# Layer 0's softmax in a two-model transformer kernel: order of evacuations, of ScalarE's shares and of the bias load

## The chip, the cores and the metric

The kernel runs on one core of a Trainium2 chip. TensorE (PE) multiplies matrices into PSUM banks, VectorE (DVE) and ScalarE (ACT) do elementwise work, GpSimd (POOL) does small work and issues some transfers, SyncE (SP) issues most transfers. All transfers share 16 DMA engines. The metric is device time of one launch in microseconds (us); a profiled execution gives the trace.

## The reference

Two small transformers run one behind the other on one sequence of 256 tokens of width 1024, two layers each. The change lies in the attention of the very first layer, so only this matters:

```python
c_act = jax.nn.silu(c)
for l in range(DEPTH):                       # DEPTH = 2
    mod = c_act @ ada_w[l] + ada_b[l]        # (1, 1024) @ (1024, 6144)
    shift_m, scale_m, gate_m, shift_f, scale_f, gate_f = ...   # six rows of 1024
    h = rms_norm(x, g_pre_mix[l]) * (1.0 + scale_m) + shift_m
    proj = h @ w_in[l] + b_in[l]             # 1280 columns: q, k, v, u
    q, k, v, u = ...                         # q and k rotated
    attn_out = sliding_window_attention_with_sinks(q, k, v, sinks[l])   # 8 heads, 2 kv heads, window 128
    pool_out = causal_pool_mixer(u, pool_w[l], pool_scale[l])
    mix = jnp.concatenate([attn_out, pool_out], axis=-1) @ w_out[l]
    x = x + gate_m * rms_norm(mix, g_post_mix[l])
    h = rms_norm(x, g_pre_ffn[l]) * (1.0 + scale_f) + shift_f
    f = (jax.nn.silu(h @ w_gate[l]) * (h @ w_up[l])) @ w_down[l]
    x = x + gate_f * rms_norm(f, g_post_ffn[l])
```

## The kernel before

Every engine has its own program, written out by hand in the order in which it is to run. Engines meet only at semaphores: `sig(name, key)` counts one up, and `wait_ge(*due(name, key))` waits for it. Nothing is reordered by a scheduler, so an instruction that waits holds up everything behind it on its engine.

**Modulation units.** A row of modulation is a product of a vector with a matrix. VectorE does it. A unit `("ada", l, n)`, called (l,n) in the text, is 256 columns of `ada_w[l]`, 1 MB, held transposed in one slot of `raw_w`; `ada(l, n)` is two instructions at L1641, each multiplying 128 columns by `c_row` and summing them (the accumulator is read by a short extra record). After n = 11, 15 and 19 a column of eight tiles is put together (L1658 and L1663 or L1664) and signals `modcol`: gate of the mixer, shift and scale of the feed-forward. For layer 0 the units come in the order (0,4) (0,0) (0,5) (0,1) (0,6) (0,2) (0,7) (0,3), then 8, 9, 10, 11, 16, 17, 18, 19, 12, 13, 14, 15, and behind them the feed-forward's weights ("gu",0,0), ("gu",0,1) and so on.

**The ring of weights.** `raw_w` has four slots. SP loads the units in this order (L1034), and before a load it waits until the unit four places earlier is done. Behind some units it also loads slices of the input weights (`ink`, L1040) and the four tiles of the output weights (`whole`, L1038: tile 2 behind (0,9), 3 behind (0,10), 0 behind (0,17), 1 behind (0,19)).

**Input products.** For every one of eight feature tiles, VectorE scales the turned input (L1842, `scaled0`), tiles 6 and 7 after (0,3). TensorE (L705) multiplies it with the input weights into six banks, (T, c) with T the half of the tokens and c a group of columns: c = 0 has 512 (q and k), c = 1 has 256, c = 2 has 512 (values and pooled features). Slices 0 to 5 go over all six banks in turn, then the last two slices product by product: (0,0) (1,0) (0,1) (1,1) (0,2) (1,2), with the transposes of the rotated q and k between (L546). VectorE adds the bias and moves each product out (`evacuate(L, T, c)`, L1853, for c = 0 and 1 with the rotation, L1863 to L1866). The scores (L504) are written to the two banks that products (0,2) and (1,2) leave.

**The bias row** `bias` (in tile `shared`, 640 KB over 128 partitions) is loaded by POOL, on a DMA queue of its own, with three small loads behind it.

**Softmax.** Six blocks of scores, n = 0 to 5. `scored(n)` on VectorE scales and masks (L1787) and takes the extreme (L1790, `smax`); `exps(n)` on ScalarE takes exponents and sums (L1301); `over_sum(n)` on VectorE takes the reciprocal of the sums (L1880); `shares(n)` on ScalarE multiplies with it (L1310, `prob`); TensorE turns the block (`turn_prob`, L546); `probT_in(n)` on ScalarE copies it out. Modulation units are put between these steps on VectorE.

**Behind it.** TensorE alternates `turn_prob(n)` and products of the pooled half with the output weights (`whole_into_y`, L595), then spreads two modulation columns over the partitions (`spread_row`, L638: gate of the mixer and scale of the feed-forward, each behind its `modcol`), does the attention outputs (L504), and the remaining output products. On ScalarE, `prepare(("gu",0,0))` (L1168) rounds the first feed-forward weights, and stands ahead of the squares of the first output rows (L1173); on VectorE `lo(("gu",0,0))` (L1628) is ahead of the first gains (L1679). Norm (L1719), transposes (L546, at `turn_norm`) and the feed-forward follow.

Of the kernel before, what the change touches and what calls it, by code (L numbers as in the profile page):

```python
# [272 lines left out]
def build(nc, counts, a_x, a_pos, a_const, const_at, a_vec, a_w, a_ink, a_whole, a_bias, a_norm, a_cnorm, a_sinks, a_gatew, a_poolw, a_c, out):  # L273
    ctx = ExitStack()
    with ctx:
# [23 lines left out]
        def due(name, *key):  # L299

            return sem(name), counts.value.get((name, *key), 1)
# [35 lines left out]
        bias, crow = shared[:, 0:1280], shared[:, 0:640]  # L337
# [122 lines left out]
        def ps(job):  # L460
            return psum[bank_of[job]]
# [586 lines left out]
        def _(pool):  # L1048
# [28 lines left out]
            def load(dst, src, n, name, *key):  # L1077
                pool.dma_start(dst, src.to_broadcast([P, n])).then_inc(*sig(name, *key, by=16))
# [30 lines left out]
                last.then_inc(*sig("sinks_set", L))  # L1109

            angles()
            pool.wait_ge(*due("ada", ("ada", 0, 7)))
            load(bias, a_bias[0:1, :], 1280, "bias_in", 0)
            pool.dma_start(sinks[:, :, :], a_sinks.rearrange("(o l) n -> o l n", o=1).to_broadcast([P, 2, HEADS])).then_inc(*sig("sinks_in", 0, by=16))
            pool.dma_start(poolw[:, 0, :, :], a_poolw[0].rearrange("g c d -> c g d")).then_inc(*sig("poolw_in", 0, by=16))
            pool.dma_start(gatew[:, :, :], a_gatew.rearrange("l g n -> g l n")).then_inc(*sig("gatew_in", 0, by=16))
# [31 lines left out]
        def _(sc):  # L1148
# [102 lines left out]
            def by_tile(bank):  # L1251
                return bank[:, :].rearrange("p (t s) -> p t s", s=P)
# [34 lines left out]
            def attention_windowed(L):  # L1287

                def qk_in(T, c):
                    dst = qk[:, 0:4, P * T:P * (T + 1)] if c == 0 else qk[:, 4, P * T:P * (T + 1)]  # L1290
                    src = by_tile(ps(("qkT", L, T, c))) if c == 0 else ps(("qkT", L, T, c))[:, 0:P]
                    copy(("qkT", L, T, c), dst, src, "qk_in", L, T, c)

                def probT_in(n):
                    copy(("probT", L, n), probT[:, n, :], ps(("probT", L, n))[:, :], "probT_in", L, n)

                def exps(n):
                    nh, w = (2, 257) if n < 4 else (4, 129)
                    sc.wait_ge(*due("smax", L, n))
                    for i in range(nh):  # L1300
                        last = nc.scalar.activation(prob[:, n, w * i:w * i + w], prob[:, n, w * i:w * i + w], ACT.Exp,  # L1301
                                                    bias=smax[:, n, i:i + 1], scale=-1.0, accum_out=ssum[:, n, i:i + 1])
                    last.then_inc(*sig("exp", L, n))

                def shares(n):
                    nh, w = (2, 257) if n < 4 else (4, 129)
                    sc.wait_ge(*due("over_sum", L, n))
                    for i in range(nh):
                        p_ = prob[:, n, w * i:w * i + w - 1]
                        last = nc.scalar.activation(p_, p_, ACT.Identity, scale=ssum[:, n, i:i + 1])  # L1310
                    last.then_inc(*sig("prob", L, n))

                def pooled_in():
                    for i in range(2):
                        copy(("pool", L, i), pooled[:, 2 * i:2 * i + 2, :].rearrange("p t s -> p (t s)"), ps(("pool", L, i))[:, :], "pooled", L, i)

                def pool_whole():
                    for i in range(2):
                        sc.wait_ge(*due("poolw", 0, i))
                        for g in range(2):  # L1320
                            t = 4 + 2 * i + g
                            last = nc.scalar.activation(raw[:, t, :], ps(("poolw", 0, i))[:, 256 * g:256 * (g + 1)], ACT.Identity,
                                                        scale=v("pool_scale0", 2 * i + g))
                        last.then_inc(*sig("pool_cat", 0, i, frees=("poolw", 0, i)))

                def pool_hi(i):
                    sc.wait_ge(*due("poolw", L, i))
                    for g in range(2):
                        t = 4 + 2 * i + g
                        last = nc.scalar.activation(in_hi[:, t, :], ps(("poolw", L, i))[:, 256 * g:256 * (g + 1)], ACT.Identity,  # L1330
                                                    scale=v(f"pool_scale{L}", 2 * i + g))
                    last.then_inc(*sig("pool_hi", L, i))

                if L == 0:

                    qk_in(0, 0)
                    qk_in(1, 0)
                    qk_in(0, 1)
                    qk_in(1, 1)
                    exps(0)  # L1340
                    exps(1)
                    shares(0)
                    pooled_in()
                    shares(1)
                    pool_whole()
                    exps(2)
                    shares(2)
                    exps(3)
                    probT_in(0)
                    exps(4)  # L1350
                    shares(3)
                    probT_in(1)
                    exps(5)
                    shares(4)
                    probT_in(2)
                    shares(5)
                    probT_in(3)
                else:
                    prepare(("in", 1, 4))
                    piece(1, "scale", 1)  # L1360
                    for T in range(2):
                        qk_in(T, 0)
                    prepare(("wo", 1, 2))
                    for T in range(2):
                        qk_in(T, 1)
                    for n in range(4):
                        exps(n)
                    probT_in(0)
                    probT_in(1)
                    prepare(("wo", 1, 3), (0,))  # L1370
                    probT_in(2)
                    pooled_in()
                    pool_hi(0)
                    pool_hi(1)
                    prepare(("wo", 1, 3), (1,))
                    exps(4)
                    exps(5)
                    probT_in(3)
                if L == 0:
                    probT_in(4)  # L1380
                    probT_in(5)
                    row_in(0, "gate", 0)
                    row_in(0, "scale", 1)
                    for jp in range(2):
                        copy(("attn", 0, jp), raw[:, 2 * jp:2 * jp + 2, :].rearrange("p t s -> p (t s)"), ps(("attn", 0, jp))[:, :], "attn_cat", 0, jp)
                    prepare(("gu", 0, 0))
                else:
                    prepare(("wo", 1, 0))
                    probT_in(4)
                    probT_in(5)  # L1390
                    prepare(("wo", 1, 1))
                    for jp in range(2):
                        sc.wait_ge(*due("attn", 1, jp))
                        nc.scalar.activation(in_hi[:, 2 * jp:2 * jp + 2, :], ps(("attn", 1, jp))[:, :], ACT.Identity).then_inc(*sig("attn_hi", 1, jp))
                        if jp == 0:
                            piece(1, "shift", 1)
                    prepare(("gu", 1, 0))
                    prepare(("gu", 1, 1))
# [202 lines left out]
        def _(ve):  # L1601
# [42 lines left out]
            def ada(l, n):  # L1644

                unit = ("ada", l, n)
                for f in range(2):
                    ada_tile(l, n, f)
                if n % 4 == 3 and not (l == 0 and n < 8):
                    ve.wait_ge(*due("ada", unit))  # L1650
                    g = n // 4
                    kind, w_ = ("shift", "scale", "gate")[g % 3], g // 3
                    mod_column(l, kind, w_, 8 * g, 0, 8, modcol[:, ROWS[(l, kind, w_)], :]).then_inc(*sig("modcol", l, kind, w_))
# [215 lines left out]
            def attention_windowed(L):  # L1869
# [12 lines left out]
                def shares(n):  # L1882
                    normalize(L, n, *((2, 256, 257) if n < 4 else (4, 128, 129)), prob, 6)
# [17 lines left out]
                if L == 0:  # L1901
                    ve.wait_ge(*due("rope1", 0))
                    ve.wait_ge(*due("bias_in", 0))
                    for c in range(2):
                        for T in range(2):
                            evacuate(0, T, c)
                    ada(0, 8)
                    evacuate(0, 0, 2)
                    evacuate(0, 1, 2)
                    ve.wait_ge(*due("const_mid", 0))  # L1910
# [1 line left out]
                    scored(0)  # L1912
                    scored(1)
                    over_sum(0)
                    ada(0, 9)
                    over_sum(1)
                    scored(2)
                    ada(0, 10)
                    over_sum(2)
                    scored(3)  # L1920
                    ada(0, 11)
                    over_sum(3)
                    scored(4)
                    ada(0, 16)
                    over_sum(4)
                    scored(5)
                    ada(0, 17)
                    over_sum(5)
                    for n in (18, 19, 12, 13, 14, 15):
                        ada(0, n)  # L1930
                    lo(("gu", 0, 0))
                else:
# [262 lines left out]
```

## Time and profile before

| | |
|---|---|
| time, median of 3 runs | 1170.52 us (1170.49 to 1171.25) |
| the profiled execution | 1170.48 us |
| its span, first to last instruction | 1168.5 us |
| TensorE busy | 1140.9 us, 98% |
| VectorE busy | 811.5 us, 69% |
| ScalarE busy | 628.0 us, 54% |
| GpSimd busy | 29.0 us, 2% |
| granted TensorE clock | 0.999 of full speed |
| DMA | 254.04 MB, mean 217 GB/s |

Shares are means over the whole span. In the first twelfth, to about 100 us, the DMA engines are full and TensorE is not; later it is the other way round. The time of the profiled execution is 1.98 us longer than its span. Times in the trace are counted from the span's start.

### The profile page before, as it was taken

Reading aid. Unit: us, or ns where it says so; the run is one execution under the profiler, and the core shown is the slowest. Engines: PE = TensorE matmul, PEld = TensorE weight load, DVE = VectorE, ACT = ScalarE, POOL = GpSimd, SP = SyncE. Lnnn points to the kernel's source line nnn. Section 1 sums busy time; section 2 is a strip of 40 time slices with the busy share of each in tenths; the row PEclk is TensorE's granted clock in tenths of the full one; section 3 lists DMA queues with packets and bytes.
Section 4 is the critical chain, followed back from the end, with each engine's and each line's share of the span. In section 5 each row is a group of like instructions: output and inputs, shape, how many; then the busy total and the mean of one; then the engine's idle time right before and its main releaser. Section 6 shows DMA issues by size and latency. Waiting matters only on the chain.

```text
span 1168.5 us, 19588 instructions
## 1 busy us (share of the span) xinstructions
PE 1140.9 (98%) x7862; PEld 1020.5 (87%) x7862; DVE 811.5 (69%) x1258; ACT 628.0 (54%) x1113; POOL 29.0 (2%) x68
## 2 busy tenths in 40 slices
PE   7999999999999999999999999999999999999997
PEld 4556999999887999999899899999989889999996
DVE  6698988776998756645677667656656866766653
ACT  3077544445566544445666766445556676655443
POOL 3100000000000000000000000000000000000000
PEclk9999999999999999999999999999999999999999
DMA  9995998887445866556343546555534435555530
GB/s 361 413 378 220 355 365 329 319 334 268 189 164 198 319 231 225 210 190 238 128 181 109 180 174 217 180 183 183 187 139 156 145 132 195 196 186 194 181 109 37
DMA packets 37996, 254.04 MB, mean 217 GB/s; under 512 B 4537, under 2 KB 4881, under 8 KB 9874
## 3 DMA queue, kind: packets, MB, share of 16 engines
q1 hardware_dynamic: 35138, 243.95, 56.6%
q0 software_dynamic: 2624, 8.84, 2.1%
q8 instruction: 63, 1.03, 0.3%
q14 instruction: 27, 0.22, 0.1%
q10 hardware_dynamic: 144, 0.00, 0.0%
HBM read 251.69 MB, written 1.08 MB: 216 GB/s over the span
## 4 chain that ended last, share of the span: by engine, by line
PE 86%; DVE 6%; ACT 3%; DMA 3%; issue 1%; SPq 0%; DVEq 0%; ACTq 0%
PE bank L497 26%; PE bank L499 25%; PE bank L498 25%; PE bank L504 3%; DMA raw_w<-weights 2%; DVE raw_w L1641 2%; PE bank L546 2%; PE bank L595 2%; ACT gtok L1173 1%; DVE lo_w L1628 1%; DMA shared<-bias_rows 1%; PE bank L946 1%; DVE tok L1853 0%; PE bank L638 0%; PE bank L897 0%
## 5 line engine op out<-in xcount | busy, mean ns | idle before, releaser
L1628 DVE TENSOR_TENSOR lo_w<-raw_w,hi_w 128x1024 fp32r<-128x1024 f32 (+3 forms) x346 | 409.4, 1209 | 122.7 <-ACT hi_w L1168 122.3
L1168 ACT ACTIVATE hi_w<-raw_w 128x1024 fp32r<-128x1024 f32 (+3 forms) x346 | 350.6, 1040 | 103.9 <-PE bank L499 89.2
L497 PE MATMUL bank<-in_hi,lo_w 128*128 128x256 f32 x1408 | 396.0, 281 | 0.0
L499 PE MATMUL bank<-in_hi,hi_w 128*128 128x256 f32 x1408 | 392.8, 279 | 0.0
L498 PE MATMUL bank<-in_lo,hi_w 128*128 128x256 f32 x1408 | 392.8, 279 | 0.0
L497 PEld LDWEIGHTS bank<-in_hi,lo_w 128*128 128x128 f32 x1408 | 264.3, 188 | 2.6 <-issue 0.8
L498 PEld LDWEIGHTS bank<-in_lo,hi_w 128*128 128x128 f32 x1408 | 263.7, 187 | 1.9 <-issue 0.5
L499 PEld LDWEIGHTS bank<-in_hi,hi_w 128*128 128x128 f32 x1408 | 264.7, 188 | 0.0
L497 PE MATMUL bank<-hi_w,hid_lo 128*128 128x512 f32 x352 | 139.6, 396 | 0.2 <-DVE hid_lo L2116 0.2
L498 PE MATMUL bank<-lo_w,hid_hi 128*128 128x512 f32 x352 | 139.0, 395 | 0.0
L499 PE MATMUL bank<-hi_w,hid_hi 128*128 128x512 f32 x352 | 139.0, 395 | 0.0
L497 PE MATMUL bank<-hi_w,in_lo 128*128 128x256 f32 (+2 forms) x432 | 130.8, 303 | 2.7 <-DVE in_lo L1738 1.6
L499 PE MATMUL bank<-hi_w,in_hi 128*128 128x256 f32 (+2 forms) x432 | 127.6, 295 | 0.0
L498 PE MATMUL bank<-lo_w,in_hi 128*128 128x256 f32 (+2 forms) x432 | 127.6, 295 | 0.0
L1641 DVE SCALAR_TENSOR_TENSOR raw_w<-raw_w,c_row 128x1024 f32<-128x1024 f32 x96 | 113.2, 1220 | 7.8 <-DMA raw_w<-weights 7.7
L497 PEld LDWEIGHTS bank<-hi_w,in_lo 128*128 128x128 f32 x432 | 81.7, 189 | 9.4 <-issue 4.1
L498 PEld LDWEIGHTS bank<-lo_w,in_hi 128*128 128x128 f32 x432 | 81.4, 188 | 2.9 <-issue 0.2
L499 PEld LDWEIGHTS bank<-hi_w,in_hi 128*128 128x128 f32 x432 | 81.3, 188 | 2.9
L1537 ACT ACTIVATE silu<-bank 128x256 f32<-128x256 f32 x44 | 16.8, 382 | 118.1 <-PE bank L499 114.3
L499 PEld LDWEIGHTS bank<-hi_w,hid_hi 128*128 128x128 f32 x352 | 66.1, 188 | 16.0
L497 PEld LDWEIGHTS bank<-hi_w,hid_lo 128*128 128x128 f32 x352 | 66.1, 188 | 14.7 <-DVE hid_lo L2116 0.6
L498 PEld LDWEIGHTS bank<-lo_w,hid_hi 128*128 128x128 f32 x352 | 66.1, 188 | 14.2
(227 smaller groups left out, 1141.1 us busy)
## 6 DMA issues: line engine op xcount, KB each, us to landing
raw_w<-weights SPq DMA_DIRECT2D x213, 1024.0 KB, 4.9
ink<-ink_w SPq DMA_DIRECT2D x8, 640.0 KB, 13.9
rows<-mod_rows POOLq DMA_DIRECT2D x7, 512.0 KB, 6.9
rows<-norm_rows POOLq DMA_DIRECT2D x5, 512.0 KB, 4.9
raw_w<-weights SPq DMA_DIRECT2D x4, 512.0 KB, 8.9
ink<-whole_w SPq DMA_DIRECT2D x2, 1024.0 KB, 22.2
early_out<-whole_w SPq DMA_DIRECT2D x2, 1024.0 KB, 7.6
raw_w<-weights SPq DMA_DIRECT2D x2, 832.0 KB, 4.5
```

What stands on the lines that cost most here:

```text
L497: nc.tensor.matmul(o, st[1], mv[0], start=start, stop=False, **kw)
L498: nc.tensor.matmul(o, st[0], mv[1], start=False, stop=False, **kw)
L499: return nc.tensor.matmul(o, st[0], mv[0], start=False, stop=stop, **kw)
L504: last = nc.tensor.matmul(o, w, r, start=(i == 0), stop=(i == len(pairs) - 1))
L546: last = nc.tensor.transpose(b[:, P * i:P * (i + 1)], s_, k("ident"))
L595: done = nc.tensor.matmul(ps(job)[:, :], half(raw[:, 2 * u + n, :], T), whole[u][:, n, cols(c)], start=(u == 2 and n == 0), stop=(u == 1 a ...
L946: nc.tensor.matmul(b[:, :], k(ones), head_sq[:, m, :], start=True, stop=True).then_inc(*sig("hsum", L, n))
L1168: nc.scalar.activation(hi_w[:, m % NSPLIT, cut], raw_view(unit)[:, cut], ACT.Identity).then_inc(*sig("hi_w", unit, i))
L1173: nc.scalar.activation(junk[:, :], src, ACT.Square, accum_out=ssq[:, T, c:c + 1]).then_inc(*sig("squared", *key, T, c))
L1537: nc.scalar.activation(silu[:, f % 2, :], src, ACT.Silu).then_inc(*sig("silu", L, f))
L1628: nc.vector.tensor_tensor(lo_w[:, m % NSPLIT, cut], raw_view(unit)[:, cut], hi_w[:, m % NSPLIT, cut].bitcast(F32), ALU.subtract).then_inc( ...
L1641: ins = nc.vector.scalar_tensor_tensor(w, w, 1.0, c_row[:, :], ALU.mult, ALU.mult, accum_out=mods[:, l, 2 * n + f:2 * n + f + 1])
```

## The change

It moves code and adds no instruction but one wait. On POOL, the bias row is loaded behind unit (0,5) instead of behind (0,7); the three small loads stay behind (0,7). On ScalarE, `shares(3)` stands ahead of `exps(4)` and `shares(4)` ahead of `exps(5)`. On VectorE, products (0,2) and (1,2) are evacuated directly behind the others, and each modulation unit between the softmax steps moves one place down: (0,8) to where (0,9) was, and so on, with (0,17) joining the row of units at the end.

```diff
@@ POOL @@
             angles()
+            pool.wait_ge(*due("ada", ("ada", 0, 5)))
+            load(bias, a_bias[0:1, :], 1280, "bias_in", 0)
             pool.wait_ge(*due("ada", ("ada", 0, 7)))
-            load(bias, a_bias[0:1, :], 1280, "bias_in", 0)
             pool.dma_start(sinks[:, :, :], a_sinks.rearrange("(o l) n -> o l n", o=1).to_broadcast([P, 2, HEADS])).then_inc(*sig("sinks_in", 0, by=16))
@@ ScalarE, attention_windowed(0) @@
                     shares(2)
                     exps(3)
                     probT_in(0)
+                    shares(3)
                     exps(4)
-                    shares(3)
                     probT_in(1)
+                    shares(4)
                     exps(5)
-                    shares(4)
                     probT_in(2)
                     shares(5)
                     probT_in(3)
@@ VectorE, attention_windowed(0) @@
                     for c in range(2):
                         for T in range(2):
                             evacuate(0, T, c)
-                    ada(0, 8)
                     evacuate(0, 0, 2)
                     evacuate(0, 1, 2)
                     ve.wait_ge(*due("const_mid", 0))
                     ve.wait_ge(*due("sinks_set", 0))
                     scored(0)
                     scored(1)
                     over_sum(0)
-                    ada(0, 9)
+                    ada(0, 8)
                     over_sum(1)
                     scored(2)
-                    ada(0, 10)
+                    ada(0, 9)
                     over_sum(2)
                     scored(3)
-                    ada(0, 11)
+                    ada(0, 10)
                     over_sum(3)
                     scored(4)
-                    ada(0, 16)
+                    ada(0, 11)
                     over_sum(4)
                     scored(5)
-                    ada(0, 17)
+                    ada(0, 16)
                     over_sum(5)
-                    for n in (18, 19, 12, 13, 14, 15):
+                    for n in (17, 18, 19, 12, 13, 14, 15):
                         ada(0, n)
                     lo(("gu", 0, 0))
```

VectorE's program before, from the last unit with rotation to the first softmax steps (L1641 is a unit, L1853 an evacuation, L1787 and L1790 a block of scores, L1880 a reciprocal; `tok` are the evacuated products):

```order
46 L1641 SCALAR_TENSOR_TENSOR raw_w,mods<-raw_w,c_row 128x1024 x2
47 L1853 TENSOR_TENSOR tok<-bank,shared 128x512 x2
48 L1787 SCALAR_TENSOR_TENSOR prob<-bank,const 128x2x256
49 L1790 TENSOR_REDUCE smax<-prob 128x2
50 L1787 SCALAR_TENSOR_TENSOR prob<-bank,const 128x2x256
51 L1790 TENSOR_REDUCE smax<-prob 128x2
52 L1880 RECIPROCAL ssum<-ssum 128x2
53 L1641 SCALAR_TENSOR_TENSOR raw_w,mods<-raw_w,c_row 128x1024 x2
```

The same place of the changed program (its lines are one higher, L1641 is L1642 there):

```order
46 L1854 TENSOR_TENSOR tok<-bank,shared 128x512 x2
47 L1788 SCALAR_TENSOR_TENSOR prob<-bank,const 128x2x256
48 L1791 TENSOR_REDUCE smax<-prob 128x2
49 L1788 SCALAR_TENSOR_TENSOR prob<-bank,const 128x2x256
50 L1791 TENSOR_REDUCE smax<-prob 128x2
51 L1881 RECIPROCAL ssum<-ssum 128x2
52 L1642 SCALAR_TENSOR_TENSOR raw_w,mods<-raw_w,c_row 128x1024 x2
```

The unit ahead of the two evacuations is gone; the unit behind the first reciprocal is now (0,8), not (0,9).

ScalarE's program before, from the exponents of block 3 (L1301 exponents, L1310 shares, L1256 a block copied out behind its transposes):

```order
20 L1301 ACTIVATE prob,ssum<-prob,smax 128x257 x2
21 L1256 ACTIVATE probT<-bank 128x512
22 L1301 ACTIVATE prob,ssum<-prob,smax 128x129 x4
23 L1310 ACTIVATE prob<-prob,ssum 128x256 x2
24 L1256 ACTIVATE probT<-bank 128x512
25 L1301 ACTIVATE prob,ssum<-prob,smax 128x129 x4
26 L1310 ACTIVATE prob<-prob,ssum 128x128 x4
```

And in the changed program:

```order
20 L1302 ACTIVATE prob,ssum<-prob,smax 128x257 x2
21 L1257 ACTIVATE probT<-bank 128x512
22 L1311 ACTIVATE prob<-prob,ssum 128x256 x2
23 L1302 ACTIVATE prob,ssum<-prob,smax 128x129 x4
24 L1257 ACTIVATE probT<-bank 128x512
25 L1311 ACTIVATE prob<-prob,ssum 128x128 x4
26 L1302 ACTIVATE prob,ssum<-prob,smax 128x129 x4
```

The shares of blocks 3 and 4 have each changed places with the exponents of the block behind.

## Rows read from the trace of the kernel before

**Rows 1.** The page: span, and TensorE's busy time, share of span, instructions.

```profile
span 1168.5 us, 19588 instructions
...
PE 1140.9 (98%) x7862; PEld 1020.5 (87%) x7862; DVE 811.5 (69%) x1258; ACT 628.0 (54%) x1113; POOL 29.0 (2%) x68
```

**Rows 2.** Chain of waits, 20 to 56 us: start us, us, what.

```profile
21.81 12.24 DMA raw_w<-weights
...
36.76 9.53 DMA shared<-bias_rows
...
51.84 2.38 DVE raw_w L1641 x4
54.22 1.21 DVE tok L1853 x2
55.43 0.24 issue
```

**Rows 3.** Timeline of VectorE: start us, us, instruction, [idle before <-releaser].

```profile
39.04 1.23 DVE L1641 SCALAR_TENSOR_TENSOR raw_w<-raw_w,c_row 128x1024 f32<-128x1024 f32 x1 [2.59 <-DMA raw_w<-weights]
...
41.92 0.73 DVE L1842 TENSOR_SCALAR raw<-raw,modcol 128x256 f32<-128x256 f32 x2
46.37 0.69 DVE L1853 TENSOR_TENSOR tok<-bank,shared 128x512 f32<-128x512 f32 x1 [3.71 <-DMA shared<-bias_rows]
...
56.91 0.69 DVE L1787 SCALAR_TENSOR_TENSOR prob<-bank,const 128x512 f32<-128x512 f32 x1 [1.49 <-PE bank L504]
...
70.13 0.16 DVE L1880 RECIPROCAL ssum<-ssum 128x2 f32<-128x2 f32 x1
...
82.45 0.17 DVE L1664 SCALAR_TENSOR_TENSOR modcol<-modcol,vcol 128x8 f32<-128x8 f32 x1
...
94.11 2.36 DVE L1628 TENSOR_TENSOR lo_w<-raw_w,hi_w 128x1024 fp32r<-128x1024 f32 x2 [2.13 <-ACT hi_w L1168]
96.39 0.68 DVE L1679 TENSOR_TENSOR gained<-bank,rows 128x512 f32<-128x512 f32 x1
...
101.01 1.41 DVE L1719 SCALAR_TENSOR_TENSOR normed<-scaled,tok_rstd,rows 128x512 f32<-128x512 f32 x2 [0.53 <-ACT tok_rstd L1185]
```

**Rows 4.** Timeline of TensorE, same columns.

```profile
25.32 22.59 PE L705 MATMUL bank<-ink,raw 128*128 128x512 f32 x64 [1.77 <-DVE raw L1842]
...
52.12 1.88 PE L705 MATMUL bank<-ink,raw 128*128 128x512 f32 x4
...
74.14 0.66 PE L546 MATMUL bank<-const,prob 128*128 128x128 f32 x4 [1.41 <-ACT prob L1310]
...
82.55 3.74 PE L638 MATMUL bank<-const,modcol 128*128 128x128 f32 x32
...
102.31 1.04 PE L546 MATMUL bank<-const,normed 128*128 128x128 f32 x8
```

**Rows 5.** Windows; at the end TensorE's clock, DMA share, GB/s.

```profile
34.00:39.00 5.00, 5.00 (x15) 2.65 (x14) 2.38 (x4) 0.00 (x0) 2.23 (x4) 1.00 1.02 417
...
62.00:64.00 2.00, 2.00 (x11) 1.63 (x10) 1.97 (x4) 2.00 (x6) 0.00 (x0) 1.00 0.65 168
...
74.00:85.00 11.00, 10.86 (x50) 6.70 (x51) 10.90 (x22) 7.66 (x24) 0.00 (x0) 1.00 1.00 375
```

**Rows 6.** Timeline of ScalarE, same columns as rows 3.

```profile
73.19 0.89 ACT L1310 ACTIVATE prob<-prob,ssum 128x256 f32<-128x256 f32 x2
...
92.95 2.00 ACT L1168 ACTIVATE hi_w<-raw_w 128x1024 fp32r<-128x1024 f32 x2 [2.99 <-DMA raw_w<-weights]
```

**Rows 7.** DMA queues, 42 to 43 us: packets, MB, share of 16 engines.

```profile
q0 software_dynamic: 33, 0.17, 41.1%
```

**Rows 8.** Timeline of SP's issues, 41 to 42 us: start us, us, issue.

```profile
41.45 0.33 SPq L1034 DMA_DIRECT2D raw_w<-weights  x1
```

**Rows 9.** DMA issues of 40 to 42 and 106 to 108 us: KB, us to landing.

```profile
raw_w<-weights SPq DMA_DIRECT2D x1, 1024.0 KB, 20.6
...
raw_w<-weights SPq DMA_DIRECT2D x1, 1024.0 KB, 4.7
```

## The prediction

> **What bounds the kernel now.** I read the page first, then the chain of waits over the stretch that the change touches, then the timelines of VectorE, TensorE and ScalarE there, then the DMA. The page has TensorE busy for 98% of a span of 1168.5 us [rows 1]: after the opening it hardly waits, so what the opening gains or loses comes out one to one at the end. The question is only when layer 0's feed-forward starts.
>
> The chain in the opening [rows 2] goes from weight DMA and modulation units to the DMA of the bias row (issued 36.76, 9.53 us), the evacuations, modulation unit (0,8), the two last evacuations (to 55.43), and the scores. On VectorE [rows 3] the reader sees the same: 3.71 us idle before 46.37 for the bias, 1.49 us before the first softmax instruction at 56.91, and then hardly a break up to the 2.13 us before 94.11. TensorE [rows 4] ran through its input products from 25.32 to 47.9 without a wait, so the bias was only one of two things that were late. It waited 1.41 us at 74.14 for ScalarE's shares of score block 3. The third party is the DMA: its 16 engines are full all through this stretch, but for 62 to 64 us (share 0.65, 168 GB/s) [rows 5]; and ScalarE waited 2.99 us, to 92.95, for the weights of ("gu",0,0) [rows 6]. So there are three paths of nearly one length, and the change moves work between them.
>
> **Part 1, bias issued after (0,5) instead of (0,7).** Unit (0,5) is done at 21.8, when SP issues its refill [rows 2]. The bias leaves then, 15 us earlier, and with the same 9.5 us is in by 31.3: its wait goes. What is late next is TensorE. Four 512-column records take 1.88 us with the last one's tail (at 52.12, [rows 4]), so 0.43 each and 0.16 of tail; a slice of all six products is 8 such and 4 of half the width, 4.3 us. From 25.32, four slices end at 42.5, and the first product's last two at 42.5 + 1.72 + 0.16 = 44.4. That would let VectorE begin 2.0 us before 46.37.
>
> But the queues are full. While the bias moved, it took 41% of the engines' time, at 0.17 MB per us [rows 7], from SP's queue, which carries the modulation weights. VectorE waits for those: 2.59 us before (0,3) at 39.04 [rows 3]. 640 KB at the 417 GB/s of this stretch [rows 5] is 1.57 us. Before, the bias traffic came after these weights; now it is ahead of them. So (0,3) starts at 40.6, tile 6 (41.92 + 0.41 = 42.3 before) is scaled at 43.9, and the first product ends at 43.9 + 1.72 + 0.16 = 45.8. VectorE starts at 45.85 instead of 46.37: **-0.5 us**, not -2.0. The three small loads behind the bias on POOL keep their place behind (0,7); they are used from 56 us on.
>
> The Trainium skill has a fit for this ("DMA: Bandwidth & Descriptors", section "Anatomy of one DMA — SWDGE (gpsimd) path"): 2.0 us fixed, and the bytes at 436 GB/s. By it the bias would cost 1.50 us instead of 1.57 and take 3.5 us to land; with the trace's 9.5 us behind full queues the second does not agree.
>
> **Part 2, last two products evacuated ahead of a modulation unit.** Before, unit (0,8) (2.38 us) stood between [rows 2], and the last product was complete at 52.12 + 1.88 = 54.0 [rows 4]. Now, from 45.6: the other three first products 3.44, two rounds of transposes 1.0, a product 1.72, transposes 0.2, the last product 1.88, together 53.85. One evacuation is 0.6 and the issue 0.24 [rows 2]: scores start at 54.8 instead of 55.67, softmax at 56.0 instead of 56.91, **-0.9 us**, part 1 included.
>
> The price: VectorE now idles for TensorE from 52.5 to 53.9 and from 54.5 to 56.0, where (0,8) used to lie. (0,8) comes behind the first reciprocal, and all units after it slip by one place. A mark on VectorE that needs a fixed number of units moves by 2.29 (one unit) - 0.9 = **+1.4 us**. The column of the second scale row, done at 82.45 + 0.17 = 82.6 before [rows 3], comes at 84.0.
>
> **Part 3, shares ahead of the next exponents.** The reciprocal of block 3 was there at 70.3 [rows 3], its shares ran only from 73.19 [rows 6], behind the exponents of block 4. Now they run from 69.1, and TensorE, which comes there at 72.7 - 0.9 = 71.8, no longer waits: **-1.41 us** at that place. Shares 4 and 5 wait for reciprocals at 73.1 and 76.8, ahead of TensorE's use at 76 and 80. But TensorE then comes early to the second scale row. Before, the gate and scale rows started at 82.55 and 84.42 (3.74 for both, [rows 4]), with 1.8 us of slack to the column at 82.6. Now TensorE would be there at 84.42 - 0.9 - 1.41 = 82.1, and the column at 84.0. So attention moves only by 84.0 - 84.42: the 1.41 us and half of part 2 go into a new wait for VectorE of 1.9 us. The compute side's sum: **-0.4 us**.
>
> **Part 4, the weight queue.** SP refills a slot of raw_w only when the unit four back is done. The refill behind (0,8) went out at 54.2; the queue still held a transfer issued at 41.45 that landed 20.6 later, at 62.05 [rows 8, 9], so it followed without a gap. Now it goes out at 56.0 + 2.65 (two blocks of softmax) + 0.08 + 2.29 = 61.0. An unqueued 1 MB lands after 4.7 us [rows 9], a queued one follows in 2.5 (at 417 GB/s): 2.2 us of lead. So the engines stand from 62.05 to 63.2 (1.1); from 65.7 to 67.0 (1.3), since the next refill goes out at 64.8; and 0.4 before the one of 72.7: 2.8 lost, against (1 - 168/417) x 2 = 1.2 before [rows 5]. From there the queue stays full in both. Some of the excess of 1.6 can be caught up, since 74 to 85 us moved 375 GB/s, not 417; nothing says how much. I take 1.2 (bounds 0 and 1.8): ("gu",0,0), landed 92.9 before, lands at **94.1**.
>
> By the skill's fit an unqueued 1 MB lands in 4.4 us, and the loss in part 4 would be 0.6 us smaller and the sum near 0; no row here shows 4.4.
>
> **Sum.** Behind this landing stand ScalarE's two roundings, VectorE's two subtractions (94.11 before) and the gain at 96.39 [rows 3]. That path moves by 1.2, less 0.1 of slack. TensorE's transposes of the first normed half at 102.31 [rows 4] stood 0.5 behind their input (norm started 101.01, [rows 3]). So they start 1.2 - 0.1 - 0.5 = **+0.6 us** later, although TensorE by itself is 0.4 earlier: the later of the two counts. From here it is one chain into the feed-forward. Profiled time 1170.48 (the span and 1.98 around it) + 0.6 = **1171.1 us**; the median of the runs, 1170.52, is only 0.04 above that execution.
>
> **The rivals.** A measurement of this kernel can tell about 0.2% from no change, 2.3 us.
> - *Weights late, nearly no change* (forecast, 0.47): 1171.1, its own range 1170.7 to 1171.9.
> - *The DMA catches up* (0.22). If the landing moves by under 0.2, the compute side decides: 1170.1. For it: the low rate from 74 to 85. Against: the share there was 1.00 [rows 5].
> - *The bias is free* (0.12). If its bytes push aside only what nobody waits for, VectorE starts 2.0 and the scores 2.2 earlier; the scale row costs 0.5 of that, and a landing still near 92.9 leaves 0.6: 1169.9, at best 1168.8. Against: the 2.59 us of waiting for (0,3).
> - *Everything adds up* (0.10), faster: no wait at the scale row, weights in time, 0.9 + 1.41 = 2.3 or a little more: 1168.0. It decides when the column is done before 82.1, for which VectorE's list is 1.9 us too long.
> - *The ring runs dry* (0.09), slower. VectorE takes the last units back to back as they land; if the four behind (0,19) each wait 0.6 us more, their refills slip too, and the landing moves by 3.6: +3.0, 1173.5. It decides from a landing 2.9 us late. Against: issues and uses move by the same 1.4.
>
> **How the numbers follow.** Faster by over 0.2% is the fourth rival, 0.10; slower the fifth, 0.09; the rest 0.81. The range spans the first three and reaches half way to the others: 1168.9 to 1172.4.
>
> **What would show it.** In the changed trace: bias traffic around 26 to 30 us; (0,3) at about 40.6; the first evacuation at 45.9 without a DMA wait; scores at 54.8, softmax at 56.0; no wait of TensorE for shares, but one of 1 to 2 us near 84 for the scale column; two dips of the DMA between 62 and 67; ("gu",0,0) rounded from about 94; the normed rows' transposes at 102.9. I am wrong if (0,3) stays at 39.0, if the later refill leaves no gap, or if the landing does not move.

## The result, and the profile after

The changed kernel takes 1172.87 us (median of 20 runs, 1171.85 to 1175.05), the kernel before 1170.97 us (20 runs of its own beside them, 1170.05 to 1172.10). The ratio is 1.0017, interval 1.0011 to 1.0023: slower by 1.9 us. The forecast was 1171.1 with a range up to 1172.4, so the time lies 0.5 us above the range, between the forecast and the rival "the ring runs dry" (1173.5), and nearer to the rival. The profiled execution took 1173.28 us with a span of 1171.3 us, 2.8 us more than before, so it is one of the longer runs; medians and marks in the trace are kept apart below. All ratios are of fast runs; of all runs reported below one was slow (4007.97 us, of the kernel with four late refills), and it is in no ratio.

VectorE's timeline in the changed kernel answers to [rows 3] (start us, us, instruction, idle before and its releaser; lines are one higher than before):

```profile
40.56 1.23 DVE L1642 SCALAR_TENSOR_TENSOR raw_w<-raw_w,c_row 128x1024 f32<-128x1024 f32 x1 [2.63 <-DMA raw_w<-weights]
...
46.09 0.69 DVE L1854 TENSOR_TENSOR tok<-bank,shared 128x512 f32<-128x512 f32 x1 [1.92 <-PE bank L705]
...
56.14 0.69 DVE L1788 SCALAR_TENSOR_TENSOR prob<-bank,const 128x512 f32<-128x512 f32 x1 [1.49 <-PE bank L504]
...
83.98 0.17 DVE L1665 SCALAR_TENSOR_TENSOR modcol<-modcol,vcol 128x8 f32<-128x8 f32 x1
84.53 1.23 DVE L1642 SCALAR_TENSOR_TENSOR raw_w<-raw_w,c_row 128x1024 f32<-128x1024 f32 x1 [0.38 <-DMA raw_w<-weights]
...
93.30 1.23 DVE L1642 SCALAR_TENSOR_TENSOR raw_w<-raw_w,c_row 128x1024 f32<-128x1024 f32 x1 [1.41 <-DMA raw_w<-weights]
...
96.95 2.36 DVE L1629 TENSOR_TENSOR lo_w<-raw_w,hi_w 128x1024 fp32r<-128x1024 f32 x2 [1.07 <-ACT hi_w L1169]
```

The first three rows are the first two parts of the change: the bias is no longer waited for (the releaser at 46.09 is TensorE), and softmax starts at 56.14 instead of 56.91. The second scale column is at 83.98, as forecast. Then two waits for modulation weights appear (84.53, 93.30) that were not there, and the subtraction of the first feed-forward weights is at 96.95, against 94.11.

TensorE's timeline answers to [rows 4]:

```profile
71.81 0.60 PE L546 MATMUL bank<-const,prob 128*128 128x128 f32 x4
73.95 3.67 PE L595 MATMUL bank<-ink,raw 128*128 128x512 f32 x8 [1.53 <-DVE prob L1788]
...
84.20 2.05 PE L638 MATMUL bank<-const,modcol 128*128 128x128 f32 x16 [0.49 <-DVE modcol L1665]
86.18 3.11 PE L504 MATMUL bank<-probT,tok 128*64 128x128 f32 x48
...
104.32 1.32 PE L546 MATMUL bank<-const,normed 128*128 128x128 f32 x8 [1.89 <-DVE normed L1720]
```

The 1.41 us wait for shares before 74.14 is gone, and 2 us further on stands one of 1.53 us for a bank. At 104.32 TensorE waits 1.89 us for the normed rows, which it did not before 102.31. ScalarE's timeline has the cause of that:

```profile
95.79 2.00 ACT L1169 ACTIVATE hi_w<-raw_w 128x1024 fp32r<-128x1024 f32 x2 [5.87 <-DMA raw_w<-weights]
```

The first feed-forward weights are rounded at 95.79, against 92.95 [rows 6]: 2.84 us later. The chain of waits (start us, us, what) between 76 and 105 us goes over it:

```profile
76.84 7.66 DMA raw_w<-weights
84.53 2.39 DVE raw_w L1642 x4
86.93 8.84 DMA raw_w<-weights
95.79 1.06 ACT hi_w L1169
96.95 1.48 DVE lo_w L1629 x2
...
103.52 0.76 DVE normed L1720
104.32 0.66 PE bank L546 x4
```

In the kernel before, the load of these weights went out at 84.93 and took 8.0 us; here it goes out at 86.93, since the unit ahead of it in its slot was itself late, and takes 8.84.

And the windows (last three columns: TensorE's clock, DMA share, GB/s) show why the weights came late:

```profile
56.00:59.00 3.00, 3.00 (x33) 2.77 (x30) 2.79 (x6) 1.18 (x5) 0.00 (x0) 1.00 1.01 421
59.00:60.00 1.00, 1.00 (x8) 0.94 (x7) 1.00 (x1) 1.00 (x5) 0.00 (x0) 1.00 0.73 303
60.00:61.00 1.00, 0.75 (x5) 0.52 (x4) 1.00 (x3) 1.00 (x4) 0.00 (x0) 1.00 0.16 66
61.00:62.00 1.00, 1.00 (x7) 0.82 (x8) 0.97 (x5) 1.00 (x3) 0.00 (x0) 1.00 0.02 8
62.00:63.00 1.00, 1.00 (x6) 0.90 (x5) 1.00 (x2) 0.99 (x4) 0.00 (x0) 1.00 0.78 164
...
65.00:66.00 1.00, 1.00 (x4) 0.51 (x3) 0.71 (x2) 0.77 (x4) 0.00 (x0) 1.00 0.64 172
66.00:67.00 1.00, 1.00 (x3) 0.38 (x2) 0.97 (x3) 0.60 (x3) 0.00 (x0) 1.00 0.53 156
...
59.00:76.00 17.00, 14.63 (x56) 8.58 (x55) 16.41 (x33) 14.48 (x47) 0.00 (x0) 1.00 0.80 292
76.00:92.00 16.00, 15.51 (x107) 10.70 (x106) 15.22 (x29) 7.11 (x16) 0.00 (x0) 1.00 1.00 413
```

The 16 engines run out of work at about 59.7 us and stand almost still until 62, and are half empty again from 65 to 67. The same two long windows of the kernel before:

```profile
59.00:76.00 17.00, 14.76 (x58) 8.80 (x58) 16.41 (x33) 12.87 (x41) 0.00 (x0) 1.00 0.97 383
76.00:92.00 16.00, 16.00 (x109) 10.88 (x108) 15.88 (x32) 8.93 (x24) 0.00 (x0) 1.00 0.99 375
```

SP's issues (start us, us, issues) say why they stood:

```profile
61.26 4.00 SPq L1034 DMA_DIRECT2D raw_w<-weights  x2
```

The refill behind (0,8) goes out at 61.26, where the kernel before had it at 54.2 [rows 2].

### The profile page after: what moved, and what is told of

Read it like the earlier page. It is cut to its first block, busy times and chain, and to the rows that moved or that the text cites. A ratio compares the mean times of both kernels' runs of the same rounds, so it can differ in the third digit from the quotient of the medians.

```text
span 1171.3 us, 19588 instructions
## 1 busy us (share of the span) xinstructions
PE 1143.8 (98%) x7862; PEld 1021.6 (87%) x7862; DVE 811.8 (69%) x1258; ACT 628.2 (54%) x1113; POOL 31.0 (3%) x68
## 3 DMA queue, kind: packets, MB, share of 16 engines
q0 software_dynamic: 2624, 8.84, 2.2%
## 4 chain that ended last, share of the span: by engine, by line
PE 85%; DVE 6%; DMA 4%; ACT 3%; issue 1%; SPq 0%; DVEq 0%; ACTq 0%
PE bank L497 26%; PE bank L499 25%; PE bank L498 25%; DMA raw_w<-weights 4%; PE bank L504 3%; DVE raw_w L1642 2%; PE bank L546 2%; DVE lo_w L1629 1%; ACT gtok L1174 1%; PE bank L705 1%; PE bank L946 1%; DVE x L1693 0%; PE bank L897 0%; DVE normed L1720 0%; DVE smax L1791 0%
## 5 line engine op out<-in xcount | busy, mean ns | idle before, releaser
L1642 DVE SCALAR_TENSOR_TENSOR raw_w<-raw_w,c_row 128x1024 f32<-128x1024 f32 x96 | 113.3, 1219 | 11.2 <-DMA raw_w<-weights 10.8
```

What stands on the lines that cost most here:

```text
L1642: ins = nc.vector.scalar_tensor_tensor(w, w, 1.0, c_row[:, :], ALU.mult, ALU.mult, accum_out=mods[:, l, 2 * n + f:2 * n + f + 1])
```

## The experiments

Each kernel was timed against the kernel before, which had 1170.81 us beside the first four, 1170.87 beside the next four, and 1170.98 beside the last three. Theory A: the change costs what the late refills of the weight ring cost, and the compute side gains next to nothing. The rivals put the loss on the early bias, on the order of the shares, or on VectorE's order as such.

**Part 2 alone** (VectorE's order; bias and shares as before):

```diff
-                    ada(0, 8)
                     evacuate(0, 0, 2)
                     evacuate(0, 1, 2)
@@ and every later unit of the softmax one place down @@
-                    ada(0, 9)
+                    ada(0, 8)
```

> The kernel before with part 2 alone: products (0,2) and (1,2) evacuated at once, every modulation unit between the softmax steps one place later; bias and shares as before. Theory A (the loss is the late refill behind (0,8), which lets the DMA run dry near 60 us): the dry gap of 60 to 62 us is there as in the changed kernel, the weights of (gu,0,0) land about 2.8 us later than 92.9, and the time is 1.7 to 2.1 us above before. Rival B (the early bias pushes the weights back and costs the time): within 0.5 us of before, since the bias is where it was.

Measured: 1172.59 us, ratio 1.0015 (1.0006 to 1.0023). The gap from 60 to 62 us is the same (66 and 8 GB/s), the first feed-forward weights are rounded at 94.87, the transposes start at 103.41. The weights are 1.9 us later than before, where 2.8 was expected; the time met the expectation. This part alone gives most of the loss, 1.8 of 1.9 us.

**Part 1 alone** (bias behind (0,5)):

```diff
-            pool.wait_ge(*due("ada", ("ada", 0, 7)))
+            pool.wait_ge(*due("ada", ("ada", 0, 5)))
             load(bias, a_bias[0:1, :], 1280, "bias_in", 0)
+            pool.wait_ge(*due("ada", ("ada", 0, 7)))
```

> The kernel before with the bias load alone moved behind (0,5). Theory A: the first evacuation starts 0.3 us earlier (46.1), unit (0,3) 1.5 us later (40.6), no dry gap of the DMA beyond that of before, (gu,0,0) still lands near 92.9; time 0 to 0.5 us below before. Rival B: the displaced weights cost 1 to 2 us at the end.

Measured: 1170.84 us, ratio 1.0002 (0.9994 to 1.0011). Unit (0,3) slips to 40.61, the first evacuation starts at 46.14 behind TensorE, softmax at 56.71 instead of 56.91. The bias is paid for in modulation weights, and 0.2 us remain at the softmax. The first feed-forward weights are rounded at 93.73, 0.8 later than before and than expected, and the time shows nothing of it.

**Part 3 alone** (shares ahead of the next exponents):

```diff
-                    exps(4)
                     shares(3)
+                    exps(4)
                     probT_in(1)
-                    exps(5)
                     shares(4)
+                    exps(5)
```

> The kernel before with part 3 alone: shares of blocks 3 and 4 ahead of the next exponents. The column of the second scale row is at 82.6 as before and TensorE comes there at 83.0, so TensorE itself is 1.4 us earlier up to the end of the output products. Theory A: (gu,0,0) lands at 92.9 as before and the path behind it has about 0.6 us of slack, so the gain is 0.4 to 0.7 us. Rival C (TensorE's own chain decides, not the weights): 1.4 us of gain.

Measured: 1170.95 us, ratio 1.0001 (0.9992 to 1.0010): neither the 0.4 to 0.7 us nor the 1.4 us of gain that were expected. TensorE's timeline of this kernel:

```profile
74.52 3.67 PE L595 MATMUL bank<-ink,raw 128*128 128x512 f32 x8 [1.54 <-DVE prob L1787]
```

The transposes of block 3 run at 72.39 without their wait, and the output products behind them then wait 1.54 us for VectorE's reading of a block of scores (L1787). These products are for the second half of the tokens and take the banks in which the scores of blocks 4 and 5 lie; block 5 is scored from 73.89 to 74.5 before the change, and without the change the products began at 74.70. The wait for shares had only covered the wait for the bank.

**The changed kernel, with one more transfer ahead of the gap**: tile 0 of the output weights is loaded behind (0,11) instead of behind (0,17), 1 MB that waits for no slot.

```diff
-WHOLE_AFTER = {("ada", 0, 9): 2, ("ada", 0, 10): 3, ("ada", 0, 17): 0, ("ada", 0, 19): 1}
+WHOLE_AFTER = {("ada", 0, 9): 2, ("ada", 0, 10): 3, ("ada", 0, 11): 0, ("ada", 0, 19): 1}
```

> The changed kernel, all three parts, with one more edit: output weight tile 0 (1 MB) is loaded behind (0,11) instead of behind (0,17), so that SP's queue holds 1 MB more when it would run dry near 60 us. VectorE's, ScalarE's and TensorE's programs are those of the changed kernel. Theory A: the gap of 60 to 62 us is mostly filled, (gu,0,0) lands within 0.6 us of 92.9 instead of at 95.8, and the time falls by 1.7 to 2.5 us against the changed kernel, to 0 to 0.5 us below before. Rival D (the later units on VectorE, by their compute, cost the time): the time stays 1.9 us above before.

Measured: 1172.14 us, ratio 1.0010 (1.0001 to 1.0018), 0.7 us below the changed kernel, which is less than was expected and, by the intervals, not clear of it. The first feed-forward weights are rounded at 94.58 (95.79 in the changed kernel). From 60 to 62 us the engines now move 426 and 377 GB/s, but later windows become emptier (213 and 180 GB/s from 65 to 67, 82 from 69 to 70): the megabyte that fills the first gap is missing behind it. From 59 to 76 us it is 307 GB/s, little more than 292. Here, filling a hole with bytes out of the same queue moved the hole.

**The kernel before, with late refills only**: SP's loads number 12 to 19 each wait for one unit of VectorE more; every other program is as before.

```diff
                     old = UNITS[n - NRAW][0]
+                    if 12 <= n <= 19:
+                        old = UNITS[n - NRAW + 1][0]
```

> The kernel before, with SP alone changed: each of the eight loads for places 12 to 19 of the ring (units (0,16) to (0,15)) waits for one modulation unit more than it needs, so it goes out about when the changed kernel sends it (62.0, 65.7, 69.8, 73.9 and so on, 0.8 to 1.0 us later still). VectorE, ScalarE and TensorE keep their programs of before. Theory A (the late refills alone make the loss): the DMA idles near 60 to 62 us, (gu,0,0) lands 2 to 3.5 us later than before, and the time is 1.7 to 3 us above before. Rival D (the loss is VectorE's and TensorE's own order): within 0.4 us of before.

Measured: 1173.59 us, ratio 1.0024 (1.0015 to 1.0033). Its windows:

```profile
59.00:76.00 17.00, 14.76 (x58) 8.79 (x57) 16.41 (x33) 12.86 (x42) 0.00 (x0) 1.00 0.77 284
76.00:92.00 16.00, 16.00 (x109) 10.91 (x108) 13.65 (x27) 8.90 (x24) 0.00 (x0) 1.00 0.99 401
```

Without any move on VectorE, ScalarE or POOL, the same gap (66 and 8 GB/s from 60 to 62), the same waits for units (84.57 and 93.20), the same late rounding (95.68) and the same late transposes (104.22, behind a wait of 1.78 us) appear. Late refills are enough for the whole loss. They cost 2.7 us here against 1.9, a difference that the intervals do not make clear; they also go out some 0.7 us later than in the changed kernel (the first at 61.98 and the third at 69.81, against 61.26 and 69.08).

**The kernel before, with one late refill**: the same edit for load 12, that of (0,16), alone.

```diff
+                    if n == 12:
+                        old = UNITS[n - NRAW + 1][0]
```

> As e5, but only the first of these loads, for unit (0,16), is held back, from 54.2 to 62.0. Theory A with the queue dry at about 59.7 us: one gap of some 3 us, but the later loads are on time and the engines catch part of it up behind it; landing 0.5 to 1.5 us later, time 0 to 1 us above before. If every later load being late matters more than the one gap, the time stays within 0.4 us.

Measured: 1170.48 us, ratio 0.9998 (0.9989 to 1.0007). Its windows:

```profile
60.00:61.00 1.00, 1.00 (x9) 0.92 (x8) 1.00 (x3) 1.00 (x5) 0.00 (x0) 1.00 0.14 57
61.00:62.00 1.00, 0.75 (x6) 0.54 (x5) 1.00 (x3) 1.00 (x3) 0.00 (x0) 1.00 0.04 16
...
59.00:76.00 17.00, 14.75 (x59) 8.96 (x58) 16.38 (x34) 12.86 (x43) 0.00 (x0) 1.00 0.81 324
76.00:92.00 16.00, 16.00 (x109) 10.86 (x108) 15.27 (x30) 9.14 (x25) 0.00 (x0) 1.00 1.01 421
```

The gap is as deep as in the changed kernel, and costs nothing: the feed-forward weights are rounded at 93.10, 0.15 later than before. What was missed is moved between 76 and 92 us, at 421 GB/s where the kernel before moved 375. The theory had expected the landing 0.5 to 1.5 us later, and less was found; the time is within the 0.4 us of the other expectation (every later load being late counts more than the one gap). The profiled execution was the longest of this kernel (1171.97). So a gap is not yet a loss.

**Four late refills**, loads 12 to 15:

> The kernel before, but only SP's loads for units (0,16), (0,17), (0,18), (0,19) each wait for one further unit of VectorE (one late load gave 1170.5 and one gap that was made up; eight late loads gave 1173.6 and an input share of 0.77 from 59 to 76 us). Theory A (the queue pays only as long as it stays shallow; once SP's issues run at four units back again, the missed megabytes come back out of the slack of 76 to 92 us): first gap at 60 to 62 us and one or two more to 68, then full; rounding of the first feed-forward weights starts at 93.5 to 94.7, time 1171.0 to 1172.0. Rival B (every gap is paid for, whatever comes later): rounding at 95.5 or later, 1172.8 to 1173.6. Rival C (four are made up like one): rounding at 93.1 or before, 1170.4 to 1170.9.

Measured: 1172.54 us, ratio 1.0017 (1.0008 to 1.0026); the rounding starts at 95.12. Its windows:

```profile
59.00:76.00 17.00, 14.76 (x59) 8.76 (x58) 16.41 (x33) 12.86 (x42) 0.00 (x0) 1.00 0.76 280
76.00:92.00 16.00, 16.00 (x109) 10.95 (x108) 13.60 (x27) 8.85 (x24) 0.00 (x0) 1.00 1.01 424
```

Neither expectation was met: I expected 93.5 to 94.7 if the missed bytes come back, 95.5 or later if they never do. The time lies between them as well (1171.0 to 1172.0, and 1172.8 to 1173.6). Part of the bytes came back, at 424 GB/s, the highest rate that any run here shows over these 16 us, and that was not enough. This gives an account in bytes against the kernel before: what is moved less from 59 to 76, minus what is moved more from 76 to 92. All rates are from the same view of the profiled executions:

| kernel | GB/s 59:76 | GB/s 76:92 | MB behind at 92 | at 421 GB/s, us | rounding later by, us |
|---|---|---|---|---|---|
| before | 383 | 375 | 0 | 0 | 0 |
| one late refill | 324 | 421 | 0.27 | 0.6 | 0.15 |
| changed, tile 0 early | 307 | 405 | 0.81 | 1.9 | 1.63 |
| part 2 alone | 301 | 400 | 0.99 | 2.4 | 1.92 |
| four late refills | 280 | 424 | 0.97 | 2.3 | 2.17 |
| changed kernel | 292 | 413 | 0.94 | 2.2 | 2.84 |
| eight late refills | 284 | 401 | 1.27 | 3.0 | 2.73 |

(Changed kernel: (383 - 292) x 17 us = 1.55 MB, less (413 - 375) x 16 us = 0.61 MB.) By the highest rate found, (424 - 375) x 16 us = 0.78 MB can be made up, 1.9 us of a full queue. The account is good to some 0.6 us for the six kernels of the table. It is worse where the queue never stands: for part 1 alone, part 3 alone and the four versions below it gives -0.5 to +0.1 us, and the rounding starts at 91.56 to 93.73, -1.4 to +0.8 us from before, off by up to 1.2 us. I have no cause for that. So the account carries the shifts of 1.6 us and more, and says nothing of smaller ones.

**The two halves of (0,8) in TensorE's gaps**: parts 1 and 3, but on VectorE only (0,8) is moved, its first 128 columns between the two last evacuations, its other 128 behind them.

```diff
-                    ada(0, 8)
                     evacuate(0, 0, 2)
+                    ada_tile(0, 8, 0)
                     evacuate(0, 1, 2)
+                    ada_tile(0, 8, 1)
```

> Parts 1 and 3 of the change, and part 2 otherwise: product (0,2) is evacuated first, then the first half of unit (0,8), then product (1,2), then the second half, so that the unit lies in the two holes in which VectorE of the changed kernel waits for TensorE (1.18 and 1.49 us). No unit behind it moves. Theory A: scores start at 55.0 as in the changed kernel, the refill goes out near 56, the DMA does not run dry, (gu,0,0) lands near 93; time 0.2 to 0.6 us below before, 2.1 to 2.5 below the changed kernel. Rival D: any order that puts work ahead of the softmax loses; above 1171.5.

Measured: 1170.29 us, ratio 0.9993 (0.9984 to 1.0002). VectorE's timeline:

```profile
52.14 0.69 DVE L1854 TENSOR_TENSOR tok<-bank,shared 128x512 f32<-128x512 f32 x1 [0.54 <-PE bank L705]
52.75 1.22 DVE L1642 SCALAR_TENSOR_TENSOR raw_w<-raw_w,c_row 128x1024 f32<-128x1024 f32 x1
...
54.01 0.69 DVE L1854 TENSOR_TENSOR tok<-bank,shared 128x512 f32<-128x512 f32 x1
54.62 1.22 DVE L1642 SCALAR_TENSOR_TENSOR raw_w<-raw_w,c_row 128x1024 f32<-128x1024 f32 x1
...
56.19 0.69 DVE L1788 SCALAR_TENSOR_TENSOR prob<-bank,const 128x512 f32<-128x512 f32 x1 [0.35 <-PE bank L504]
```

Softmax starts as early as in the changed kernel (56.19 against 56.14), and (0,8) is done too, in the two gaps in which the changed kernel idled. The refill goes out at 55.87, the queue stays full (390 GB/s from 59 to 76), TensorE does not wait for the scale column, the weights are rounded at 92.70, near the 93 expected, and the transposes start at 101.55. Against the changed kernel, the evacuations are nearly as early and the units are back in their places: the loss goes with the late refills.

**The same, with tile 0 of the output weights early as well:**

> e7 with output weight tile 0 loaded behind (0,11) as in e4, which fills the dip of the DMA at 62 to 64 us that the kernel before has too. Theory A: (gu,0,0) lands 0.5 to 1.2 us earlier than in e7, TensorE's own chain, 0.8 us ahead of before, then decides; time 0.6 to 1.0 us below before.

Measured: 1169.73 us, ratio 0.9991 (0.9982 to 1.0000). The reason expected for it is not in the trace: the weights are rounded at 93.63, 0.9 later than in the version before it and not 0.5 to 1.2 earlier, though this was the longest execution of this kernel (1170.93). It was run once more beside the same kernel without the early bias:

> The version with the two halves of unit (0,8) around the last evacuations, shares ahead, early bias, and tile 0 of the output weights loaded behind (0,11), timed once more beside its neighbour: 1169.5 to 1170.1, 0.9991 of the kernel before, within 0.0009 of it.

> The version with the two halves of unit (0,8) around the last evacuations, shares ahead, and tile 0 of the output weights loaded behind (0,11), but with the bias row loaded behind (0,7) as before. Theory A (the early bias saves 0.5 us on VectorE's start and is worth a few tenths of that at the end): first evacuation at 46.4, softmax 56.7 instead of 56.2, time 1170.0 to 1170.4. Rival B (it is worth nothing, since the weights of the feed-forward set the end): within 0.1 of the version with the early bias. Rival C (it costs, since its bytes push the weights aside): below that version by 0.3 or more.

Measured: 1170.31 us, 0.9993 (0.9984 to 1.0002), with the early bias, above the 1169.5 to 1170.1 expected, and 1170.14 us, 0.9994 (0.9986 to 1.0003), without. No worth of the early bias can be seen at the end: without it softmax starts at 56.00, no later than with it (56.07), since the last products of TensorE set that start in both. The expectation that it would be 56.7 was wrong: it took the 56.91 of before to hang on the bias, and it hung on (0,8) standing ahead of the evacuations. The best of these versions are 0.6 to 1.1 us below the kernel before, at the edge of what can be told, and 2.6 to 3.1 us below the changed one.

## Why the prediction was wrong

**Parts 1 and 2, right in size.** Forecast and trace agree within 0.3 us at five marks: (0,3) at 40.6 and 40.56, first evacuation 45.85 and 46.09, scores 54.8 and 54.91, softmax 56.0 and 56.14, scale column 84.0 and 83.98. While the bias moved, one window shows it taking half of the engines' time:

```profile
q0 software_dynamic: 41, 0.21, 51.3%
```

That is at 26 to 27 us of the changed kernel, where the text expected it (packets, MB, share); SP's queue moved 40 packets beside these 41. The Trainium skill says that each DMA engine takes turns between the queues that have work, packet by packet ("DMA: Bandwidth & Descriptors", section "Queues, rings and completion order"), and this half agrees.

**Part 3, a gain that was not there.** The step that failed is "TensorE no longer waits: -1.41 us at that place". The wait for shares did go, but the same program position needed a bank that VectorE frees at the end of scoring block 5, 73.14 + 0.66 = 73.8 in the changed kernel, and the products start at 73.95; before, it was 73.89 + 0.66 = 74.55, and 74.70. The distance is 0.15 us in both. The sum was hardly hurt, since the prediction lost this gain again in a wait for the scale column: it forecast 1.9 us there, and found 0.49. Attention starts at 86.18 where 85.8 was forecast. Two errors of opposite sign met.

**Part 4, the step that decided.** The issue times were right (refill behind (0,8) forecast 61.0, found 61.26). Wrong was the sentence "the engines stand from 62.05 to 63.2 (1.1)". I had read the landing of the last queued load at 62.05 [rows 8, 9] as the time to which the queue had work. It is the time at which the whole of that load had landed; in the kernel before the engines had by then moved most of the load behind it (410 to 426 GB/s from 59 to 62). The changed kernel has nothing behind it, and its 16 engines run out of work at 59.7. The hint stood in [rows 5]: with 1 MB still to move after 62.05, the kernel before could not have dipped to 168 GB/s from 62 to 64. Forecast were 2.8 us of standing, 1.6 more than before, with 0.4 of it caught up. By the rates, at 421 GB/s for a full queue, the changed kernel stood 2.7 us from 59 to 63 where 1.1 was forecast, 1.2 from 65 to 67 where 1.3 was, and 1.3 in the rest of the stretch where 0.4 was: the first gap began at 59.7 and not at 62.05, and its end near 63.2 was right. In all, found were 3.7 us more than before from 59 to 76 us (1.55 MB at 421 GB/s), of which 0.61 MB, 1.4 us, were caught up; the weights came 2.84 us later, not 1.2. The slack behind them was right: 2.84 less 0.6 is 2.2, and the transposes are 2.0 us later (104.32 against 102.31), VectorE's first subtraction of hidden values in the feed-forward 2.3 (133.69 against 131.40), and the time 1.9.

So the mechanism ("weights late") was the right one, and its size was wrong by 1.6 us: the term of the sum that failed is the landing's move, 1.2 us with a bound of 1.8, and 2.84 measured. Within it, the 4.7 us for an unqueued load held (the refill of 61.26 took 4.7); the 4.4 that the prediction worked out beside it from the fit in the Trainium skill ("DMA: Bandwidth & Descriptors", section "Anatomy of one DMA — SWDGE (gpsimd) path") is for loads that GpSimd issues, and these are SP's. The rival "the ring runs dry" had this size (a landing 3.6 us later), but for another reason: waits of each of the last units. Two such waits exist (84.53, 93.30; 1.8 us together), and the first does put back the load of the feed-forward weights, as that rival has it (86.93 against 84.93; 1.4 of these 2.0 us are the forecast slip by one unit). The four late refills have two as well, with every load behind them issued by the old rule, so these waits come with the missing bytes. I have not separated how much of the last 0.6 us (2.84 against 2.2 in the account) they add.

"The DMA catches up" was half right: it does, by up to 0.78 MB, because the kernel before moves 375 GB/s from 76 to 92 us where others move up to 424. What sets this rate no run separates. "The bias is free" is refuted by (0,3) at 40.56, in the part 1 kernel at 40.61.

## What to carry to other kernels

Where a ring of buffers is refilled only when a consumer is done, moving that consumer down is a change to the transfer schedule first: count the bytes queued at the moment at which the refill used to go out, the bytes that the stretch behind can make up at the full rate, and the slack of the first thing that waits for the last of them (0.6 us here); what exceeds these is paid. A landing tells when the last byte of a load was in, so the end of a queue's work is read from the windows. Before a wait is booked as a gain, look at the next instruction on that engine and ask what its operands and its bank would have waited for; and put the moved work into the gaps that the move opens, rather than behind them.

## What the runs showed of the hardware

The last load of the full queue in the changed kernel went out at 42.97 and landed after 18.9 us, at 61.9:

```profile
raw_w<-weights SPq DMA_DIRECT2D x1, 1024.0 KB, 18.9
```

In the two microseconds from 60 to 62 the 16 engines together moved 66 and 8 GB/s, 0.07 MB. So a landing came 2.2 us after nearly all of the bytes. The Trainium skill says that each of the 16 engines counts its own share up when it is through ("DMA: Bandwidth & Descriptors", section "Why a DMA increments its semaphore by 16 and not by 1"). The trace agrees for the first part of the 2.2 us, in which the rate runs down from 164 GB/s (59.7 to 60) to 66 (60 to 61), as when few engines are left. The last 0.6 us and more are without any data:

```profile
61.25:62.00 0.75, 0.75 (x6) 0.57 (x5) 0.72 (x3) 0.75 (x3) 0.00 (x0) 1.00 0.00 0
```

No view here shows the engines one by one, so that the slowest one set the landing is argued and not shown.

A gap of about 3 us in the middle of a stream cost nothing that could be measured (1170.48 against 1170.87 us), and the queue moved 421 GB/s afterwards instead of 375, both at a share of 0.99 or more of the engines' time. A busy share near 1 does not mean that no more can be moved: the share is the time of packets, and a packet took 0.31 us on average in the one case and 0.28 in the other (76 to 92 us; 825 and 930 packets). A high share with few bytes is also seen at the start of a single load on idle engines (kernel before, 107.0 to 107.5 us: share 1.21, 164 GB/s). It may be that the kernel before has such starts between 76 and 92 us too (76.5 to 77.0: 1.45, 246 GB/s); no run tests it.
